# A 20-slot ring laid over the mixer's buffers, in a fused decoder block on one core

## The reference: what is computed

```python
h = rms_norm(x, g_mix_norm);  proj = h @ w_in            # 1024 x 7168
# retention (8 heads of 128, chunks of 128) and a pooling mixer (windows 2, 4, 8, 16)
merged = sigmoid(gate_a) * (y_ret @ w_branch[0]) + sigmoid(gate_b) * (y_pool @ w_branch[1])
x = x + merged @ w_out
h2 = rms_norm(x, g_ffn_norm)
logits = h2 @ w_router + b_router                        # 32 experts, top 4, softmax over the 4
gu = h2[rows of expert e] @ w_gate_up[e] + b_gate_up[e]  # 1024 x 2048
act = (clip(up, -7, 7) + 1) * (g * sigmoid(1.702 * g)),  g = min(gate, 7)
x = x + sum over chosen experts of weight * (act @ w_down[e] + b_down[e])   # 1024 x 1024
x = x + sigmoid(rms_norm(x, g_ple_norm) @ w_ple_gate) * (p @ w_ple_proj)    # "embedding", p is 256 x 256
y = rms_norm(x, g_final)
```

## Time and profile before

| | |
|---|---|
| median of three executions | 1264.03 us |
| the profiled execution | 1262.35 us |
| its span, first to last instruction | 1260.5 us |
| mean granted TensorE clock | 0.977 |
| TensorE busy (matmuls) | 1156.8 us, 92% |
| VectorE, ScalarE busy | 391.9 us, 201.3 us |
| bytes moved | 456.98 MB, mean 363 GB/s |

### The profile page before, as it was taken

The page is one execution under the profiler, slowest core; times in us unless marked ns, Lnnn a source line. Parts: engine busy times, 40 slices in busy tenths (PEclk is TensorE's granted clock), DMA queues, the critical chain, the costliest instruction groups (busy, mean ns, idle before and its releaser), DMA issues.

```text
span 1260.5 us, 13315 instructions
## 1 busy us (share of the span) xinstructions
PE 1156.8 (92%) x5340; PEld 599.4 (48%) x5341; DVE 391.9 (31%) x620; ACT 201.3 (16%) x267; POOL 8.0 (1%) x19
## 2 busy tenths in 40 slices
PE   7999999989998989889999998998989998989787
PEld 5888888863343433333333433342433433333236
DVE  6964755631030312212221212130303122121126
ACT  5354444320000000000000000000000000000024
POOL 0000000000000000000000000000000000000000
PEclk9999999999899999999999999999998999999999
DMA  9855455769699999999899999999999999999970
GB/s 344 296 169 164 137 196 194 284 258 384 274 428 427 427 430 427 429 427 428 363 428 429 428 428 428 427 428 427 428 427 428 391 429 429 427 429 427 428 311 34
DMA packets 56089, 456.98 MB, mean 363 GB/s; under 512 B 5342, under 2 KB 6796, under 8 KB 30252
## 3 DMA queue, kind: packets, MB, share of 16 engines
q1 hardware_dynamic: 53740, 451.98, 86.9%
q10 hardware_dynamic: 2304, 4.37, 1.0%
HBM read 455.28 MB, written 1.05 MB: 362 GB/s over the span
## 4 chain that ended last, share of the span: by engine, by line
PE 57%; DMA 39%; DVE 2%; issue 1%; SPq 1%; ACT 0%; DVEq 0%; POOLq 0%; POOL 0%; ACTq 0%
PE ps L563 55%; DMA ring<-in_w_down 21%; DMA ring<-in_w_gate_up 18%; PE ps L570 1%; PE ps L829 1%; SPq L477 0%; SPq L472 0%; DMA x<-in_x 0%; PE ps L845 0%; DVE B L1481 0%; DVE over_xn L1272 0%; ACT B L1148 0%; DVE B L1494 0%; DVE x L1409 0%; DVE B L1490 0%
## 5 line engine op out<-in xcount | busy, mean ns | idle before, releaser
L563 PE MATMUL ps<-ring,B 128*64 128x512 f32 x3040 | 685.4, 607 | 71.7 <-DMA ring<-in_w_gate_up 47.6
L563 PEld LDWEIGHTS ps<-ring,B 128*64 128x64 f32 x3040 | 233.2, 140 | 509.8 <-issue 507.1
L1485 DVE TENSOR_SCALAR B<-ps 128x1024 f32<-128x1024 f32 x16 | 19.6, 1225 | 462.5 <-PE ps L563 462.5
L563 PE MATMUL ps<-w_split,over_hT 128*128 128x512 f32 x480 | 153.4, 396 | 2.7 <-DVE w_split L1264 2.7
L1264 DVE TENSOR_TENSOR w_split<-ring,w_split 128x1024 fp32r<-128x1024 f32 x80 | 96.3, 1224 | 68.6 <-ACT w_split L1022 68.3
L1139 ACT ACTIVATE B<-B 128x1024 f32<-128x1024 f32 x16 | 16.9, 1057 | 598.7 <-DVE B L1485 598.7
L563 PEld LDWEIGHTS ps<-w_split,over_hT 128*128 128x128 f32 x480 | 90.9, 191 | 21.7 <-issue 3.1
L563 PE MATMUL ps<-w_split,over_xn 128*128 128x512 f32 x256 | 100.7, 393 | 0.0
L1022 ACT CAST w_split<-ring 128x1024 fp32r<-128x1024 f32 x80 | 83.2, 1055 | 103.2 <-PE ps L563 103.2
L563 PE MATMUL ps<-B 128*128 128x512 f32 (+3 forms) x280 | 90.3, 497 | 2.2 <-ACT B L1148 1.2
L563 PEld LDWEIGHTS ps<-B,xn 128*128 128x128 f32 x512 | 62.8, 200 | 13.3 <-issue 13.3
(11 more groups left out here) (151 smaller groups left out, 462.8 us busy)
## 6 DMA issues: line engine op xcount, KB each, us to landing
ring<-in_w_gate_up SPq DMA_DIRECT2D x120, 2048.0 KB, 17.1
ring<-in_w_down SPq DMA_DIRECT2D x64, 2048.0 KB, 17.1
ring<-in_w_in SPq DMA_DIRECT2D x28, 1024.0 KB, 5.2
ring<-in_w_gate_up SPq DMA_DIRECT2D x12, 1024.0 KB, 9.4
ring<-in_w_branch SPq DMA_DIRECT2D x8, 1024.0 KB, 6.9
ring<-in_w_out SPq DMA_DIRECT2D x4, 1024.0 KB, 5.1
B<-in_w_gate_up SPq DMA_DIRECT2D x4, 1024.0 KB, 6.3
ring<-in_w_ple_gate SPq DMA_DIRECT2D x4, 1024.0 KB, 16.4
```

Source lines behind the costliest of these rows:

```text
L563: return pe.matmul(out, lhsT, rhs, start=start, stop=stop, skip_group_check=True)
L1485: step(ve.tensor_scalar(gate, two_banks(0), LIMIT, None, ALU.min), s.gate_ready)
```

## The change

- The ring has 20 slots (`SLOTS`). Slots 12 to 19 are the former B8, B7, B2, B4, B6, B3, B5 and hT; only B0 and B1 stay buffers of their own. In the mixer these eight slots are used as before under their old names. In the expert part the ring has ten places for 2 MiB chunks instead of six.
- The class `Ring` works out, when the program is built, into which place each of the 184 big loads goes and at which count of used chunks it is free. Its free list begins with places 8 and 9 (slots 16 to 19), which hold no fine chunk: the first two big loads can go before any fine chunk is used. The others take the place that was freed longest ago. The last four down loads may only take places 0, 1, 6 and 7 (`LAST_DOWN`).
- From turn 12 on place 9 is given to the embedding: `w_ple_proj` and `p` are loaded into it by SP's queue, between big loads, and the projection's result is written over the weights.
- The routing tables, the router's weights, the scatter matrices and the transposed `p` lie over the mixer's constants.
- VectorE's and ScalarE's buffers of the expert part shrink: the sigmoid is written over the gate, so it waits until (up+1)*gate is formed; the scattered rows take the place of `up`, so ScalarE's copy of them waits for the activation.
- The extra work stands behind turns 11 (routing), 12 (output bias) and 13 (embedding). All turns are written out; there is no `Fori` over turns.

```diff
-SLOTS, SLOT = 12, 2048
+SLOTS, SLOT = 20, 2048
-EMBED_TURN, ROUTE_TURN, BIAS_TURN = 5, 8, 11
+ROUTE_TURN, BIAS_TURN, EMBED_TURN = 11, 12, 13
+MIXER_BUFFERS = (8, 7, 2, 4, 6, 3, 5, "hT")
+FINE_UNITS = (12, 13, 14, 15, 0, 1, 2, 3, 8, 9, 10, 11, 4, 5, 6, 7)
+LATE_PLACES = (8, 9) if UNITS == 2 else (4,)
+LAST_DOWN = (0, 1, 2, 3, 12, 13, 14, 15)
+class Ring:
+    def __init__(self):
+        free = [(0, at) for at in LATE_PLACES]
+        free += [(f + UNITS, FINE_UNITS[f] // UNITS) for f in range(0, FINE, UNITS)]
...
+        for g in range(BIGS):
+            if self.retired is None and g >= (EMBED_TURN - 2) * PER_TURN and free[0][1] == PLACES - 1:
+                self.retired = (g, free.pop(0)[0])
+            last = g >= BIGS - DOWNS
+            taken = next(i for i, (_, at) in enumerate(free) if not last or UNITS * at in LAST_DOWN)
+            value, at = free.pop(taken)
...
+            if not last:
+                free.append((FINE + g + 1, at))
...
+            def load_big(pair, q, down):
+                g = chunk_number(pair, q, down)
+                if g >= len(LATE_PLACES):
+                    sp.wait_ge(used, RING.free_at[g])
...
+            sp.wait_ge(pool_psum, 4)
+            load_fine(12)
             load_early(5)
             sp.wait_ge(piece_used, PARTS * (BRANCH + 3))
-            load_fine(12)
+            load_fine(14)
+            load_fine(15)
...
             sp.wait_ge(branch_read, 4)
+            if UNITS == 2:
+                load_big(1, 0, False)
             load_early(4)
+            for unit in (8, 9, 10, 11, 6, 7):
+                load_after_piece(unit)
+            sp.wait_ge(logitT_psum, 1)
+            for q in range(len(LATE_PLACES) - 1, UPS):
+                load_big(1, q, False)
...
-                nc.scalar.activation(sig, gate, ACT.Sigmoid, scale=ALPHA).then_inc(s.sig_ready, 1)
+                nc.scalar.activation(gate, gate, ACT.Sigmoid, scale=ALPHA).then_inc(s.sig_ready, 1)
...
                 sigmoid(first, turn)
+                e.wait_ge(first.act_ready, 2 * turn + 2)
                 read_down(first, turn - 1)
...
-            with e.Fori(2, EMBED_TURN) as turn:
+            for turn in range(1, PAIRS):
                 pair_turn(turn)
...
-                step(ve.tensor_scalar(gate, two_banks(0), LIMIT, None, ALU.min), s.gate_ready)
+                step(ve.tensor_scalar(gate, two_banks(0), LIMIT, None, ALU.min))
...
-                step(ve.scalar_tensor_tensor(up, up, 1.0, gate, ALU.add, ALU.mult))
+                step(ve.scalar_tensor_tensor(up, up, 1.0, gate, ALU.add, ALU.mult), s.gate_ready)
```

More of the change, by code:

```diff
@@ L292, in build @@
         more = ExpertSemaphores(sem, "more")
-        used, loaded = first.chunk_used, first.loaded
-        fine_loaded = mixer_loaded + [sem(f"fine_loaded{i}") for i in range(MIXER_SLOTS, SLOTS)]
+        used = first.chunk_used
+        loaded = [sem(f"loaded{i}") for i in range(PLACES)]
+        fine_loaded = mixer_loaded + [sem(f"fine_loaded{i}") for i in range(MIXER_SLOTS, FINE)]
+        gate_loaded = [sem(f"gate_loaded{i}") for i in range(len(PLE_RAW))]
         block = ctx.enter_context(nc.Block())
@@ L332, in big_slot, with chunk_number @@
[L332 to L337, removed]
+            return s is first and pair == 0
+        def chunk_number(pair, q, down):
+            turn = pair + 1 if down else pair
+            if turn == PAIRS:
+                return (PAIRS - 1) * PER_TURN + q
+            return (turn - 1) * PER_TURN + (UPS if down else 0) + q
@@ L339, in up_weights, with place_of, place @@
+        def place_of(s, pair, q, down):
+            if s is first:
+                return RING.place[chunk_number(pair, q, down)]
+            return ((UPS if down else 0) + q) % MORE_PLACES
+        def place(at):
+            return ring[:, UNITS * at:UNITS * (at + 1), :].rearrange("p a n -> p (a n)")
         def up_weights(s, pair, h, c):
             if is_fine(s, pair):
-                return fine_slot(2 * c + h)
-            return big_slot(2 * (c // 2) + h)[:, (c % 2) * SLOT:(c % 2 + 1) * SLOT]
+                return ring[:, FINE_UNITS[2 * c + h], :]
+            at = place_of(s, pair, 2 * (c // UP_ROWS) + h, False)
+            return place(at)[:, (c % UP_ROWS) * SLOT:(c % UP_ROWS + 1) * SLOT]
@@ new lines, in load_big, with load_embedding @@
+            def load_big(pair, q, down):
+                g = chunk_number(pair, q, down)
+                if g >= len(LATE_PLACES):
+                    sp.wait_ge(used, RING.free_at[g])
+                if down:
+                    load_down(RING.place[g], q // 2, 2 * pair + q % 2)
+                else:
+                    load_up(RING.place[g], q // 2, 2 * pair + q % 2)
+            def load_embedding():
+                sp.wait_ge(used, RING.retired[1])
+                sp.dma_start(w_proj, t["w_ple_proj"][0].rearrange("(c p) n -> p c n", p=P)).then_inc(proj_loaded, 16)
+                sp.dma_start(p_in, t["p"][0, 0].rearrange("(i p) n -> p i n", p=P)).then_inc(p_loaded, 16)
@@ L521, in _ @@
-            with sp.Fori(2, PAIRS) as turn:
-                for q in range(PER_TURN):
-                    sp.wait_ge(used, PER_TURN * turn + q + FINE - PER_TURN - BIGS + 1)
-                    load_turn(q, turn)
-            for q in range(KD // 2):
-                sp.wait_ge(used, PER_TURN * (PAIRS - 1) + q + FINE - BIGS + 1)
-                load_down(first, q, q // 2, N_EXPERTS - 2 + q % 2)
+            for unit in (8, 9, 10, 11, 6, 7):
+                load_after_piece(unit)
+            sp.wait_ge(logitT_psum, 1)
@@ L826, in act_to_width @@
                 for half in range(2):
[L827 removed]
+                    pe.wait_ge(s.act_ready, 2 * pair + (half + 1 if DOWN_ROWS == 4 else 2))
                     for j in range(4):
[L829 removed]
+                        c = 4 * half + j
+                        start = DOWN_ROWS * P * (c // DOWN_ROWS)
+                        last = pe.transpose(ps[:, 6 + half, j * P:(j + 1) * P],
+                                            gate[:, start + c % DOWN_ROWS:start + DOWN_ROWS * P:DOWN_ROWS], ident)
                     last.then_inc(s.act_xposed, 1)
```

333 lines of the change are left out of this document (156 added, 177 removed).

## The result

The changed kernel takes 1245.84 us (median of four executions, 1244.77 to 1247.41) against 1264.05: ratio 0.9857, 95% interval 0.9846 to 0.9869, so 18.2 us less. 1243.8 us was predicted, range 1237 to 1251. The profiled execution took 1246.63 us, its span 1244.8; the two profiled executions are 15.7 us apart (1262.35 and 1246.63), so their traces account for less than the medians do.

What follows compares the result with a forecast made beforehand. Weight transfers were taken as the bound. 9.8 + 8.2 + 7.7 - 3.1 - 2.0 - 0.4 = 20.2 us earlier gave 1242.2 profiled; with 1.7 for the median, 1243.8 us, range 1237 to 1251.

Steps and rivals of the forecast that it cites:

- The bound: Expert part: weight transfers at 428.5 GB/s set the pace, 58.73 us a turn; TensorE has 6.5 us to spare.
- Two chunks ahead, 9.8: Before the expert stream: places 8 and 9 filled early leave 182 chunks to stream, 9.8 us less.
- the hole behind pair 0, 8.2: Stream at 315 to 335 us: eight places filled instead of six shrink the hole from 14.0 to 5.8 us.
- The extra work, 7.7: Behind embedding and output bias: a deeper queue closes both holes in the stream, 7.7 us less.
- The last down chunks, 2.0: End of the stream: the last two loads wait for pair 14's down products, 2.0 us lost, bounds 0 and 5.
- The embedding's bytes, 3.1: Late turns: 1.05 + 0.26 MB now stand in a full stream, 3.1 us more.
- Turns written out, 0.4: Expert part without loops: 0.2 MB more code fetched, 0.4 us more, bounds 0 and 1.
- the constant 5.3: Whole stream: remainder of the check on the kernel before, for start and trailing packets, kept unchanged at 5.3 us.
- A: Holes at the end and behind pair 0 gone, embedding bytes absorbed: 1237 us; chance 0.12.
- B: Chunks put ahead not free, their gain halved, or TensorE late after turns 11 to 13: 1249 to 1253 us; chance 0.12.
- C: Whole stream: no change, the ring only shifts where transfers wait: 1262 to 1266 us; chance 0.03.
- D: Written-out turns: code fetch waits behind queued chunks, slower, up to about 1377 us; chance 0.03.

Runs made afterwards that it cites:

- the repeat: The changed kernel, unaltered, measured once more on the chip of some experiments: 1245.44 us, ratio 0.9860 to the kernel before.
- before_sig_late: The kernel before, with only ScalarE's sigmoid made to wait until (up+1)*gate is formed: 1265.19 us, ratio 1.0007.
- chain_plus4: The changed kernel with four more VectorE clamps of up ahead of (up+1)*gate in every turn: 1249.09 us, ratio 0.9890.
- the limit: The changed kernel, but SP issues a big load only when the third one before it has landed: 1245.17 us, ratio 0.9850.

## Why the prediction was right, and where it was off

**The bound.** Right: the stream sets the pace in both kernels (58.7 us a turn), and the gain came from bytes ahead and from holes. The ring of six places in the changed code shows it from the other side: without the depth the rest of the change costs 6.5 us (1271.29 against 1264.81).

**What part was luck.** The sum was for the landing of the last chunk. It came 14.9 us earlier (1197.69 against 1212.56), not 20.2. The profiled execution was forecast at 1242.2 and took 1246.63, 4.4 more; 1.7 of that is the slow clock at pair 14 that the repeat does not have. The median is off by 2.0 only, because I had added 1.7 for a median above the profiled execution, as in the kernel before, and this time the median lies 0.8 below it. So the terms below explain the trace, and the good agreement of the median is partly luck.

**Two chunks ahead, 9.8, and the hole behind pair 0, 8.2.** Together nearly right in size: the chunks were ahead and the hole went from 14.0 to 7.0 us. The sum did not count anything twice, but it gave each term a worth that it has only beside the other. Filling the two places ahead is worth only 2.4 us when they could be filled behind pair 0 instead. What counts is that ten places are filled before TensorE frees the next one; the ring of eight puts the last two places at 10.3. From six places to ten, 25.8 us (24.7 with each against the kernel before on its own chip) stand against 9.8 + 8.2 + 7.7 = 25.7 forecast.

**The hole itself** was 7.0 us instead of the 5.8 predicted. First transposes at 317.71 instead of 316.36 us, 1.35 later, were forecast (1.1); the first freed place was not. SP's timeline of the changed kernel, beside the earlier trace rows:

```profile
305.89 26.32 SPq L516 DMA_DIRECT2D ring<-in_w_down  x4
```

Its last issue is at 305.89 + 26.32 - 0.33 = 331.88, 2.9 later than 328.95 before, where 1.1 was forecast. The wait of TensorE before the transposes grew from 3.3 to 4.5 us, and the granted clock stayed at 0.50 from 320 to 325 us, where it had been 0.75: the first quarter of pair 1's products ran at 1.2 GHz for longer. So the delay was paid again as slow clock. This is not a fixed surcharge: in `before_sig_late` 1.55 us at the transposes became 2.7 at the issue, in `chain_plus4` a further 2.9 became only 1.5.

**The extra work, 7.7.** Right: no dips, with ten places as with eight, and no effect of where it stands. No wait for weights grew beyond 2.8 us, and the last chunks were still waited for, so TensorE was not late at the end for it.

**The last down chunks, 2.0.** Right as far as the time resolves it: 1.75 when they no longer wait.

**The embedding's bytes, 3.1,** were not tested alone. In the changed kernel's chain the turn that holds them takes 997.74 - 935.71 = 62.03 us instead of 58.73, 3.3 more.

**Turns written out, 0.4, and the constant 5.3: the step that failed.** The last chunk of pair 14 landed at 1175.65; my terms give 1192.4 - 2.0 - 4 x 4.894 = 1170.8. Of the 4.8 us, 1.2 are the hole. The rest is in the stream, for which I had no term but a constant. In the chain of the changed kernel, 12 chunks take 58.7 us again and again, but 60.3 from 560.61 to 620.90 (579.22 + 41.68), 60.0 from 757.95 to 817.96 and 60.0 from 997.74 to 1057.73: 4.1 us in three steps. The kernel before has no such step between 660.72 and 954.88 us, nor between 1016.68 and 1183.13. The byte count says the same in another way. By the time of the landing at 1175.65 this had been moved:

```profile
DMA packets 26321, 376.83 MB, mean 423 GB/s; under 512 B 2887, under 2 KB 3143, under 8 KB 3399
q1 hardware_dynamic: 26284, 376.27, 99.6%
```

376.27 less 1.31 MB of the embedding is 178.79 chunks, where 178 had to be there: the landing trails by 0.79 of a chunk, 3.9 us. By the same count in the kernel before it was 0.45 chunk at 508.87 us (89.03 MB), 0.46 at 1016.68 (302.95 MB), and 0.34, or 1.6 us, at its last chunk (386.58 MB less 184 chunks). That last value is in the 5.3 that I had carried over as a constant, so the trailing took 2.3 us more. And 376.83 MB in 1175.65 - 285.1 - 1.9 - 7.0 = 881.7 us are 427.4 GB/s, not the 428.5 of my sum, 2.2 us. Of these 0.8 were in the constant too: before, 388.00 MB in 1212.56 - 285.1 - 1.9 - 19.3 = 906.3 us are 428.1 GB/s. With the hole this makes 1.2 + 2.3 + 1.4 = 4.9 us. What makes the landings fall behind is not the depth of the queue, as the limit showed. The instruction queue moved 11 packets more than before (20 in the earlier trace rows). Queues of the changed kernel, 285 to 1196 us, beside the earlier trace rows:

```profile
q8 instruction: 31, 0.51, 0.2%
```

31 blocks in 911 us are one in 29.4 us, and eight of them are 235 us, close to the 240 us between the steps above. The steps also stand in the six-place ring, whose turns are written out as well (six chunks in 30.84 and 30.81 us instead of 29.37, 236 us apart). That each block holds up one of the DMA engines that share every chunk, and that the engine which is last already is hit at every eighth, would fit these numbers. It is a guess: no run kept the loops with the deep ring, so it is shown only that the steps come with the changed code at six places as at ten, and that the kernel before does not have them; the cause stays open. The bytes of the code, 0.2 MB, were forecast rightly.

**The rivals.** A needed the holes behind pair 0 and at the end gone and the embedding's bytes absorbed; none of the three came. B's premise was wrong: nothing was moved from 276 us until the stream began at 285, so the fine loads and both chunks had landed. C and D did not happen: behind pair 0 TensorE's waits for anything but weights are the 4.5 us at pair 0's activation and four single ones of 0.9 to 1.6 us.

## What to carry to other kernels

When a stream of weights is the bound, count free places at the moment the consumer pauses, not only bytes ahead: depth is worth what it lets the queue carry over the longest gap between two frees. A place filled earlier is not there to close the hole later, so the two gains are priced together. A step on another engine that is hidden 15 times may be paid once, at the first turn where nothing stands beside it; reordering two operations there gave back 1.9 us, more than the sigmoid's own 1.1. When places are kept for a later user, check that the last loads do not have to wait for the few that are left.

## What the runs showed of the hardware that I had not expected

- Landings can fall behind a full-rate stream in steps (1.4 us, 240 to 241 us apart) that no slice of GB/s shows as a dip, and are not made good by the landings behind them. The depth of the queue, three or eight chunks of 2 MiB, changed neither this nor the time (1245.17 and 1245.44 us).
- SyncE's issue of a 2 MiB load took 0.33 to 0.38 us with at most three chunks in flight and up to 4.8 us in the changed kernel, where a chunk landed up to 42.9 us, nearly nine chunks' time, after its issue. The longer issues cost nothing here, since the time of the two kernels is the same.
- Two profiled executions of the same kernel differ by 2.5 us in their spans (1242.3 and 1244.8), 1.7 of it because the granted clock fell to 1.2 GHz in pair 14's last down products in one and not in the other, behind the same wait of 2.68 us.
- TensorE's slow clock behind pair 0 ended at about 327 us both when its products there began at 321.62 and when they began at 324.53 us, so how much of a delay comes through is not fixed.
